# Part of the modulation product taken from TensorE to VectorE, and the tail of both attentions laid on one table of steps

## What is computed

```python
sh1, sc1, g1, sh2, sc2, g2 = [m[:, None, :] for m in
                              jnp.split(jax.nn.silu(c) @ w_ada + b_ada, 6, axis=-1)]
...
h_l = modulate(rms_norm(x, norm1_w), sh1, sc1)
...
def gla_out(o, r):
    return from_heads(rms_norm(o, gla_onorm_w)) * jax.nn.silu(r)
...
q_l = rope_2d(diff_qk(dq_l, diff_qnorm_w), ang_row, ang_col)
k_l = rope_2d(diff_qk(dk_l, diff_knorm_w), ang_row, ang_col)
...
a = p[:, :, 0] - lam * p[:, :, 1]
...
def merge(h, ya, yb):
    g_a, g_b = jnp.split(jax.nn.sigmoid(h @ w_gate + b_gate), 2, axis=-1)
    return (g_a * (ya @ w_proj_gla) + g_b * (yb @ w_proj_diff)) @ w_out

x_new = x + g1 * mix_l
```

## Time and profile before

| | |
|---|---|
| median of three runs | 2606.09 us (2604.33 to 2609.31) |
| profiled execution, its own time | 2608.7 us |
| profiled execution, span | 2606.6 us |
| TensorE busy, share of the span | 2449.8 us, 94% |
| VectorE busy, share | 1296.0 us, 50% |
| ScalarE busy, share | 1068.2 us, 41% |
| mean granted TensorE clock | 0.972 of full |
| moved from memory | 456.56 MB, mean 175 GB/s |

### The profile page before, as it was taken

How to read it: one execution, slowest core, us unless ns; L and a number is a source line. 1 busy time by engine, 2 the same in 40 slices (tenths; PEclk the granted TensorE clock), 3 DMA queues, 4 the chain that set the end, 5 groups by cost and what they waited for, 6 DMA issues and landing times.

```text
span 2606.6 us, 38153 instructions
## 1 busy us (share of the span) xinstructions
PE 2449.8 (94%) x16127; PEld 2084.3 (80%) x16127; DVE 1296.0 (50%) x1780; ACT 1068.2 (41%) x1449; POOL 43.4 (2%) x53
## 2 busy tenths in 40 slices
PE   5779999999977999998999999999999999999998
PEld 1346677899856788866999988899988899999886
DVE  1122222359545545545655565566666544366654
ACT  3223323345433553334444443344454544244433
POOL 2000000002000000000000000000000000000000
PEclk8889999999989999999999999999999999999999
DMA  8664666245332336776577765655655566333354
GB/s 291 216 198 151 214 217 217 83 135 147 106 105 92 119 122 204 240 248 203 187 228 230 230 217 189 190 182 183 186 169 191 162 194 195 102 111 122 112 166 151
DMA packets 255434, 456.56 MB, mean 175 GB/s; under 512 B 20947, under 2 KB 49937, under 8 KB 253984
## 3 DMA queue, kind: packets, MB, share of 16 engines
q1 hardware_dynamic: 252672, 442.47, 54.1%
q0 software_dynamic: 2016, 7.46, 0.8%
q10 hardware_dynamic: 576, 4.19, 0.4%
HBM read 451.97 MB, written 2.10 MB: 174 GB/s over the span
## 4 chain that ended last, share of the span: by engine, by line
PE 85%; DVE 4%; DMA 4%; ACT 3%; DVEq 1%; issue 1%; ACTq 0%; SPq 0%
PE psum L588 72%; PE psum L657 4%; DMA sbuf<-in_w_ada 3%; DVE fast L1777 2%; PE psum L565 2%; ACT fast L1223 1%; PE psum L1076 1%; PE psum L889 1%; PE psum L840 1%; DVE fast L1797 1%; PE psum L1106 1%; DMA sbuf<-in_w_proj_diff 1%; PE psum L667 1%; PE psum L787 1%; PE psum L906 0%
## 5 line engine op out<-in xcount | busy, mean ns | idle before, releaser
L588 PE MATMUL psum<-fast,fast 128*128 128x256 f32 (+3 forms) x13680 | 2090.8, 313 | 29.9 <-DVE fast L1777 23.9
L588 PEld LDWEIGHTS psum<-fast,fast 128*128 128x128 f32 (+2 forms) x13680 | 1888.9, 191 | 251.6 <-issue 87.2
L1777 DVE TENSOR_TENSOR fast<-sbuf,fast 128x1024 fp32r<-128x1024 f32 (+3 forms) x655 | 783.0, 1199 | 1097.7 <-ACT fast L1223 1091.7
L1223 ACT ACTIVATE fast<-sbuf 128x1024 fp32r<-128x1024 f32 (+3 forms) x655 | 674.2, 1033 | 1132.5 <-PE psum L588 1003.3
L1223 ACT ACTIVATE sbuf<-psum 128x512 f32<-128x512 f32 (+5 forms) x236 | 112.1, 496 | 247.0 <-PE psum L657 121.9
L657 PE MATMUL psum<-sbuf 128*32 128x512 f32 x768 | 148.9, 662 | 34.3 <-DMA sbuf<-in_w_ada 34.3
L657 PEld LDWEIGHTS psum<-sbuf 128*32 128x32 f32 x768 | 21.1, 112 | 96.8 <-DMA sbuf<-in_w_ada 71.3
L565 PE MATMUL psum<-sbuf,sbuf 128*128 128x128 f32 (+2 forms) x317 | 57.9, 295 | 27.6 <-DMA sbuf<-in_consts 10.3
L565 PEld LDWEIGHTS psum<-sbuf,sbuf 128*128 128x128 f32 (+2 forms) x317 | 38.7, 148 | 54.5 <-issue 19.1
L1797 DVE TENSOR_TENSOR fast<-sbuf,fast 128x512 fp32r<-128x512 f32 (+2 forms) x63 | 58.0, 920 | 4.7
L1795 DVE CAST fast<-sbuf 128x512 fp32r<-128x512 f32 (+2 forms) x63 | 33.9, 538 | 28.6 <-ACT sbuf L1311 24.7
(11 more groups left out here) (229 smaller groups left out, 942.0 us busy)
## 6 DMA issues: line engine op xcount, KB each, us to landing
sbuf<-in_w_ada SPq DMA_DIRECT2D x192, 512.0 KB, 4.6
sbuf<-in_w_up SPq DMA_DIRECT2D x176, 512.0 KB, 4.0
sbuf<-in_w_in SPq DMA_DIRECT2D x158, 512.0 KB, 3.8
sbuf<-in_w_down SPq DMA_DIRECT2D x88, 512.0 KB, 4.3
sbuf<-in_w_gate SPq DMA_DIRECT2D x64, 512.0 KB, 3.6
sbuf<-in_w_out SPq DMA_DIRECT2D x64, 512.0 KB, 4.9
sbuf<-in_w_proj_gla SPq DMA_DIRECT2D x16, 512.0 KB, 4.5
sbuf<-in_w_proj_diff SPq DMA_DIRECT2D x16, 512.0 KB, 5.6
```

The lines of the kernel that those rows point to most:

```text
L588: last = mm(out, lhsT, rhs, start=first and key not in opened, stop=end, skip_group_check=True)
L1223: return A(out, in_, ACT.Copy, scale=scale)
L1777: last = tt(lo, raw, hi.bitcast(F32), ALU.subtract)
```

## The change

**Modulation.** Chunks now have one of three kinds. Parts 0 to 7 stay plain. The chunks of parts 8 to 23 are of kind 2: they are not multiplied by TensorE. VectorE multiplies each of the two row tiles by its column of `silu(c)` and adds it to a running sum of 128 x 512 (`sum_chunk`), and this releases the slot. `Stream.beside` replaces `paired`: single chunks, three to two split chunks through the first 43 chunks of gv0 to dv1, one in 1.875 through pg0 to out3, one in 2.5 in the `w_up` stretch, starting at its fifteenth chunk. `sum_chunk` is called right after `rest_chunk`, so VectorE takes the chunks in the order of the ring. There are two sum tiles (`rows`), used in turn, so part a may start when part a - 2 is folded. The folds stay on TensorE, with ones in place of the row selectors, and ScalarE's copies of the sums for these parts are gone. Only the first vector's product is formed for parts 8 to 23.

```diff
-        self.paired([("gv0", panel("w_in", 1024, 512)), ("gv1", panel("w_in", 1536, 512)),
+        self.beside([("gv0", panel("w_in", 1024, 512)), ("gv1", panel("w_in", 1536, 512)),
...
-                     ("dv0", panel("w_in", 5152, 512)), ("dv1", panel("w_in", 5664, 512))], ada, range(8, 16), 1, 1)
+                     ("dv0", panel("w_in", 5152, 512)), ("dv1", panel("w_in", 5664, 512))], ada, range(8, 16), 2, 3)
...
-                    + [(f"out{n}", panel("w_out", 512 * n, 512)) for n in range(4)], ada, range(16, 20), 15, 4)
+                    + [(f"out{n}", panel("w_out", 512 * n, 512)) for n in range(4)], ada, range(16, 20), 15, 8)
...
-        self.paired(ups[:KFA // 2], ada, range(20, 24), 5, 1, 16)
+        self.beside(ups[:KFA // 2], ada, range(20, 24), 5, 2, 14)
...
             def modulation(s):
                 if s in st.fold_at:
                     ada_fold(st.fold_at[s])
-                if s in st.rows_at:
-                    a, i = st.rows_at[s]
-                    ada_chunk(a, i)
-                    ada_chunk(a, i + 1)
...
+            def sum_chunk(a, i):
+
+                g = st.job[f"ada{a}"][i]
+                if i == 0:
+                    dve.wait_ge(S("ada_folded"), max(a - 1, 8))
+                dve.wait_ge(S(st.landed(g)[0]), st.landed(g)[1])
+                w, sums = ring(g), rows[a % 2]
+                for j in range(2):
+                    k = 2 * i + j
+                    if k == 0:
+                        last = ts(sums, w[:, j, :], csil[:, k, 0:1], None, ALU.mult)
+                    else:
+                        dve.drain()
+                        last = stt(sums, w[:, j, :], csil[:, k, 0:1], sums, ALU.mult, ALU.add)
+                last.then_inc(S("modulation_summed"), 1)
+
             def modulation(s):
+                for a, i in st.sums_at.get(s, ()):
+                    sum_chunk(a, i)
```

```diff
+GLA_OUT, DIFF, MIX_STEPS = 30, 48, 96
...
+            def logs(out, sums, n):
+
+                return A(out, sums, ACT.Ln, scale=1.0 / n, bias=small[:, 7:8])
+
+            def roots_of(x):
+                return A(x, x, ACT.Exp, scale=-0.5)
...
+                    if a in (6, 7):
+                        b = a - 6
+                        act.wait_ge(S("gla_summed"), b + 1)
+                        logs(tmp[:, 1024 * b:1024 * b + 1024], banks(4 + 2 * b), P).then_inc(S("gla_logs"), 1)
+                    if a in (9, 10):
+                        b = a - 9
+                        act.wait_ge(S("qk_summed"), 5 + b)
+                        logs(qsq[b], banks(4 + 2 * b), 64)
+                    if a in (11, 12):
+                        act.drain()
+                        roots_of(qsq[a - 11]).then_inc(S("qk_roots"), 1)
...
+                    if n % 2 == 1 and 0 < n < 33:
+                        diff_exps(n // 2)
```

More of the change, by code:

```diff
@@ L210, in __init__, with add @@
             self.add(f"o2{n}", panel("w_out_2", 512 * n, 512))
-        self.split = [g for g, plain in enumerate(self.plain) if not plain]
-    def add(self, name, chunks, plain=False):
+        self.split = [g for g, kind in enumerate(self.kind) if not kind]
+    def add(self, name, chunks, kind=0):
         for c in chunks:
@@ L242, in before @@
         for job in self.job:
-            if self.plain[self.job[job][0]]:
+            if self.kind[self.job[job][0]]:
                 continue
@@ L395, in build @@
         wup = Y(11280 + 1024, 2, 512)[0:32, :, :]
-        rows = Y(13328, 512)
+        rows = [Y(13328, 512), Y(22176, 512)]
         dk = Y(13984, 8, 2, T)
@@ L666, in ada_fold @@
                     for m in range(4):
-                        last = mm(bank(5, 2 * m, 2), rows[:, m * P:(m + 1) * P], C("rowsel"), start=True, stop=True)
+                        if a < 8:
+                            last = mm(bank(5, 2 * m, 2), sums[:, m * P:(m + 1) * P], C("rowsel"), start=True, stop=True)
+                        else:
+                            last = mm(bank(5, 2 * m, 1), sums[:, m * P:(m + 1) * P], C("ones")[:, 0:1], start=True, stop=True)
                 else:
@@ L777, in context_states, with key_norms @@
                 yield
-            def qk_norms(first, last):
-                for g in range(first, last):
+            def key_norms():
+                for g in range(4):
                     yield
@@ L1507, in _, with gates_out @@
                 act.drain()
-            for n in range(8):
-                steps(f"gate{n}")
+            def gates_out(n):
                 if n == 0:
-                    act.wait_ge(S("gla_out_ready"), 4)
+                    act.wait_ge(S("gr_gated"), 2)
                 if n == 4:
-                    act.wait_ge(S("yg_ready"), 1)
+                    act.wait_ge(S("qk_done"), 6)
                 for b in range(2):
@@ L1520, in _ @@
                     last.then_inc(emptied, 1)
+            pending = None
+            for name in ["gq", "gr0", "gr1", "dq0", "dq1"] + [f"gate{n}" for n in range(8)]:
+                for q, g in enumerate(st.job[name]):
+                    if (name, q) == ("gq", 6):
+                        side = mixers()
+                    round_chunk(st.nth[g] + 2)
+                    if q == 0 and pending:
+                        (columns_out if pending in ("gr0", "gr1", "dq0", "dq1") else gates_out)(
+                            int(pending[4:]) if pending[0:4] == "gate" else pending)
+                    next(side, None)
+                if name == "gq":
+                    columns_out(name)
+                else:
+                    pending = name
             for _ in side:
                 pass
+            gates_out(7)
             for k in ("pg", "pd"):
```

483 lines of the change are left out of this document (257 added, 226 removed).

## The result

The change makes the kernel faster: 2486.77 us in the median of 4 runs (2486.40 to 2489.68), against 2605.21 us in the median of the 4 runs of before that go with it. The ratio is 0.9549, 95% interval 0.953 to 0.9568. The forecast was 2480, with a range of 2462 to 2500 for its own case.

The account below looks back on a forecast made before the run. TensorE, busy 94% of the span and 85% of the chain of waits, was taken as the bound. Savings of 27 + 67 + 16 + 16 = 126 from 2606.1 gave 2480 us, own range 2462 to 2500, overall 2458 to 2522.

Parts of the forecast that it names:

- Price of a summed chunk: VectorE, all summed stretches: two instructions of 0.75 us, each followed after 0.08, make 1.66 us a chunk, 212 for 128.
- the rival that instructions follow late: VectorE's chained sum instructions each wait 0.48 us, not 0.08, so a chunk costs 2.5 us; total 2507 us, chance 0.10.
- gv0 to dv1: First stretch: 32 plain pairs removed save 32 us, 3 and 2 given back around the gate logits; net -27, bounds -20 and -31.
- Rest of both attentions: Stretch 683 to 1000 us: 244 us of work remains if waits go, 8 charged for late steps; net -67, bounds -50 and -75.
- Reason (2): Differential attention: exponentials come a step (2.88 us) earlier, ending the score product's 1.63 us wait; units shrink from 9.14 to 8.1.
- reason (1): Attention norms: 1.28 us table loads and 2048-wide passes delay rests by 3.93 us and rotation by 6.22; smaller steps remove this.
- pg0 to out3: Stretch 1000 to 1225 us: 16 pairs and 9 us of idle and clock saved, traffic +2, merge 7 late; net -16, bounds -5 and -26.
- my slower rival: The ring of four slots starves because a slot's cycle, with sums ahead, is too long: 2666 us, slower than before; chance 0.04.
- The 7 us for VectorE's merge in pd: In the four pd jobs VectorE needs 13.7 us a job against TensorE's 11.5, so some 7 us is late overall.
- `w_up`: Its first part: removing 16 pairs at 0.99 us gives -16, with VectorE at 240 of 294 us; bounds -6 and -16.
- Half table: Attention links still arrive after the step that asks, units stay at 9.14 us and the mixers give 30: 2517 us, chance 0.13.
- Starving ring: Four slots carry the chunks only while cycle C stays below 9.1, 7.5 and 8.1 us by stretch; C = 10.7 costs 186; chance 0.04.

## Why the prediction was right, and where it was not

**Price of a summed chunk: right.** 0.75 us an instruction and 0.83 from start to start, 1.66 a chunk. The Trainium skill ("VectorE: DVE Perf Modes", section "The DRAIN you can't avoid") would have an estimated 1.24 from start to start if its flush comes on top of the recorded duration; the trace has 0.83, so here it does not, and the rival that instructions follow late falls. The section itself adds that a next operation that is not held, that is, not made to wait for every earlier one to finish, starts earlier.

**gv0 to dv1: right, 25.2 for 27, with two sizes off that cancel.** The place was the one named, the step with the scans: TensorE waits 3.33 us there, and 3.97 instead of 2.64 at the end of gv0. Both were charged. Not charged was the clock behind them, 4.9 us (below). On the other side the pairs gave more than 32. The price of 1.00 us was the pair's own row, between chunks of 5.67; without pairs five chunks follow each other in 27.46 us, 5.49 each:

```profile
302.49 27.46 PE L595 MATMUL psum<-fast,fast 128*128 128x512 f32 x120
```

So a pair had cost 1.00 and what it added to the chunk beside it, 5.67 - 5.49 = 0.18, together 1.2 us. The 32 pairs gave some 36 us: TensorE is busy 31.5 us less in spite of the 4.9 of slow work. That the sum of this stretch came out nearly right is partly luck.

**Rest of both attentions: right in size, 70.3 for 67, with one reason that stops a link short.** The count of what remains if every wait goes, 244, lies within 3 us of the 246.7 measured, and the 8 us for unseen waits were not needed. Reason (2), "the new table puts the exponentials of unit u a step earlier", is true as far as it goes, but the step that counts is that of the maxima: putting the exponentials alone back costs 3.6 us, and putting the whole chain back from the maxima on costs 22.5. I had read who was waited for (ScalarE's exponentials) and not what they had waited for: VectorE's maxima, for which ScalarE stood 2.12 us at each unit. The table loads of reason (1) count for nothing by themselves (1.0 us). Most of the gain is not in the units at all. Up to the first score product, before and after:

```profile
683.00:789.60 106.60, 75.35 (x482) 64.48 (x482) 47.13 (x35) 45.19 (x48) 0.00 (x0) 0.87 0.30 94
...
655.30:717.40 62.10, 62.10 (x456) 56.23 (x456) 30.76 (x27) 33.91 (x37) 0.00 (x0) 1.00 0.46 136
```

That is 44.5 of the 70.3 us, about 3 of it one chunk that now comes behind this point; 31.3 us are waits of TensorE that are gone, and the clock rose from 0.87 to 1.00. The units and the output norm share the remaining 26. What makes up the 44.5 was not taken apart: halves, logs that read PSUM directly, the earlier `tanh` and the deferred copies came together, and no run undoes one of them alone. So for the larger part of this stretch the cause is argued and not shown.

**pg0 to out3: wrong in size, 5.3 for 16.** The failed step is "of the idle 9.75 and the clock's 4.5 I let 9 go", with "+2" for the traffic. The mechanism was the one of my slower rival, in this one stretch. DMA issues of the changed kernel there, with KB each and median us to landing:

```profile
sbuf<-in_w_out SPq DMA_DIRECT2D x32, 512.0 KB, 5.6
sbuf<-in_w_ada SPq DMA_DIRECT2D x31, 512.0 KB, 5.0
```

A landing takes 5.0 to 5.6 us; with 1.07 and 1.23 that is 7.3 to 7.9, at a limit of 7.5 for 1.53 slots per chunk. So stalls grew by 11 us instead of going, and the clock fell to 0.95. I had both numbers, and put them under a rival of 0.04 instead of into the sum. That the ring is the cause rests on the run with parts 16 and 17 moved, where 16 slots fewer take 13 of the 21 us of waits away; that it is the slot's turn and not something else in the transfers is argued. The 7 us for VectorE's merge in pd was too much: spreading it gives 2.3, or 3.8 by the stretch. Yet TensorE's waits at the ends of pd0 to pd3, 4.1, 3.3, 1.5 and 4.7 us, are more than the "some 2 us a job" of the forecast.

**`w_up`: the gain is larger, 19.6 for 16.** VectorE is busy 231.3 of 290.4 us where the forecast was 240 of 294, and TensorE does not wait for a rest; its only wait is one of 7.2 us that was there before. So the mechanism was right, and the mis-sized term is again the pair: 19.6 us for 16 pairs is 1.2 each and not 0.99, which put the favourable bound of 16 too low. The cover has an end not far above, as the doubled sums show.

The total is near because the errors cancel in part: 3.3 us more than forecast in the attentions, 3.6 in `w_up` and 1.8 outside the stretches, against 10.7 less from pg0 to out3 and 1.8 less from gv0 to dv1.

**The rivals.** Half table: no, units last 8.3 us on average (7.44 and 9.16 in turn). Starving ring: only in pg0 to out3, and there worth 11 us and not 186, as if C were a little above its limit of 7.5 and not at 10.7. My reading is that the sums of the chunks ahead mostly run while the transfer is still under way; no run shows it by itself.

## What to carry to other kernels

Work that is moved to an idle engine takes that engine's time and, where it reads from a ring of buffers, a slot for as long as it waits its turn. Compare slots per step, divided by the slots of the ring, times the whole cycle of a slot (landing, each reader's turn) with the time of a step, stretch by stretch, and move the extra chunks to where that product is small, even if they are needed much later. And where an engine waits for another at each turn of a loop, follow the wait one more link back before saying which step has to move.

## What the runs showed of the hardware

A wait of TensorE can cost more than its length. The changed kernel's stretch behind the wait of 3.33 us, then that behind the wait of 3.97 us:

```profile
251.50:262.30 10.80, 10.73 (x29) 7.08 (x30) 5.73 (x8) 2.81 (x5) 0.00 (x0) 0.68 0.76 243
...
272.70:284.00 11.30, 11.25 (x43) 9.14 (x44) 8.55 (x12) 3.37 (x5) 0.00 (x0) 0.85 0.46 140
```

The granted clock is 0.68 and 0.85 there, so part of the time at 1.2 instead of 2.4 GHz; the chunk behind the first wait takes 8.01 us instead of 5.74. In the kernel before, the wait of 2.64 us at the same place is followed by a chunk of 5.68 us:

```profile
275.80:288.00 12.20, 12.18 (x56) 9.19 (x57) 9.32 (x13) 3.83 (x6) 0.00 (x0) 1.00 0.55 188
```

There the clock stayed at 1.00. The waits differ by 0.7 us and the slow work behind them by 3 us, but the length of the wait alone does not decide it: with the maxima late, one of 2.07 us was followed by a chunk of 4.63 us where 3.14 is usual, at a granted clock of 0.89 from 725.9 to 741:

```profile
725.90 1.13 PE L898 MATMUL psum<-sbuf,sbuf 64*128 64x512 f32 x4 [2.07 <-ACT sbuf L1464]
726.96 4.63 PE L595 MATMUL psum<-fast,fast 128*128 128x256 f32 x24
```

What else decides is not shown here. The price can be counted, though. Removing the waits of 3.33 and 3.97 us together gave 11.7: 6.9 us of idle time, and 4.9 us by which the work behind the two waits was slower (the gate logits 2.93 for 1.98 us, one chunk 8.01 for 5.74, five chunks 29.09 for 27.46).
